# Expert weights in loads of 4 MB: slots side by side in one tensor, gate and up rows 4p + r

## The chip, the cores and the metric

One Trainium2 chip, one NeuronCore of it. Everything is fp32. The metric is the device time of one launch in microseconds, median of several runs; below, 1176.56 us for the kernel before.

## What is computed

One layer of a decoder for 256 tokens of width 1024: a combined input projection, sparse attention and a convolution branch, their mix, a layer norm, then a mixture of 32 experts of which each token takes 4, and a last gated embedding with a layer norm. The change touches the experts:

```python
def moe_ffn(h, w_router, b_router, w_gate_up, b_gate_up, w_down, b_down):
    ...
    top_vals, top_idx = lax.top_k(logits, TOP_K_EXPERTS)          # 4 of 32
    for e in range(N_EXPERTS):
        gu = t @ w_gate_up[e] + b_gate_up[e]                       # (1024, 2048)
        g, u = gu[:, :D_EXPERT], gu[:, D_EXPERT:]
        ...
        act = (u + 1) * (g * jax.nn.sigmoid(SWIGLU_ALPHA * g))
        y = act @ w_down[e] + b_down[e]                            # (1024, 1024)
        out = out + combine[:, e:e + 1].astype(t.dtype) * y
```

An expert's weights are 8 MiB of gate and up and 4 MiB of down, 384 MiB for all of them, each read once.

## The kernel before

**Stages.** The front (projection, attention, convolution, mix, router) reads its own weights through a ring of 12 chunks of 1 MiB (`ring`, `FRONT`, `w_view`, lines 287 to 313). Then the experts run one after the other, and last the gated embedding and the second layer norm.

**Slots.** An expert's weights come as six pairs of chunks (`CPE = 6`) of 2 MiB: c = 0 to 3 are 256 rows each of gate and up, c = 4 and 5 are 512 rows each of down. There are `ES = 11` slots of 2 MiB. Slots 0 to 5 are two chunks of `ring` each, slots 6 to 10 lie in `arena` (`extra`, at `EX + PAIR * (0, 1, 2, 4, 3)`), where the front's tensors lie before. The list in lines 323 to 332 hands slots out in a fixed turn, so load n takes the slot of load n - 11 (`last_in`); load `PP` has no bytes, and a slot is kept for a result there.

**Rows.** In `pair_source` (line 344) partition p gets rows 2p and 2p + 1 of a pair's 256 rows of gate and up, 16 KB that lie together, and rows 4p to 4p + 3 of 512 of down, also 16 KB.

**The gather.** Tokens of an expert are picked by a product with a one-hot matrix. The weights of these matmuls are columns of `x1`, in the order in which the rows of the expert's weights lie on the partitions: `x1_rows` (line 381) takes `x1` as 4 blocks of 128 x 2, so each weight load reads every second column. `gather` (line 399) does it for two experts at once, 16 matmuls, which are 32 records in the trace, after every odd expert; `first_gather` (line 408) for the first two experts, in pieces spread over the end of the router's work and expert 0; line 1170 for an expert with more than 64 tokens (two rounds).

**Who issues the loads.** SP's queue, in program order. While the front runs, `early` and `into_ring` (lines 563 to 597) fill the eleven slots as the front's tensors and chunks come free: load 9 ahead of chunk 25, then 0, 6, 1, half of 10, 2, 7, 3, 8, 4, 5 and the other half of 10. From line 604 on load n waits until TensorE has read load n - 11 (`pair_read`) and is issued; the loads in `PIECES` come in 2 or 4 parts as parts of the slot come free. `LAST` and the very last down pair are split too (lines 349 to 361). Each slot has a semaphore (`e_in`), and `filled[n]` is the count at which load n is there; TensorE waits for it in `pair` (line 949).

**TensorE in an expert** (`one_round`, line 1118): 64 records of gate and up (16 a pair), turning the sums, adding the last expert's rows to the total (`combine`, line 441), turning the gates or, after an odd expert, the next gather, and 32 records of down. `product` (line 423) issues both kinds. In experts 28 and 30 two embeddings (`embed`) lie between.

## Time and profile before

| | |
|---|---|
| three runs | 1176.01, 1176.56, 1176.84 us, median 1176.56 |
| the profiled execution | 1175.06 us |
| its span, first to last instruction | 1173.2 us |
| granted TensorE clock | 0.998 of full |
| TensorE matmul / weight load busy | 98% / 50% of the span |
| VectorE, ScalarE, GpSimd busy | 25%, 15%, 1% |
| DMA, packets of SP's queue | 90.8% of 16 engines' span |
| bytes | 448.16 MB, mean 382 GB/s |

A busy share is an average over stages with different limits, and matmuls are pipelined, with modelled ends: TensorE at 98% may still be waiting for short times between matmuls. Load and store shares say how full the 16 DMA engines were. What bounds a stage is read from that stage.

### The profile page before, as it was taken

How to read it: one execution, taken by the hardware profiler on the slowest of the kernel's cores; microseconds unless marked ns; L12 is line 12 of the kernel's file. 1: busy time of each engine (PE TensorE's matmuls, PEld its weight loads, DVE VectorE, ACT ScalarE, POOL GpSimd, SP SyncE). 2: the span in 40 equal slices, each digit the busy share in tenths (PEclk: the TensorE clock that was granted, in tenths of full speed). 3: DMA queues.
4: the chain of work that ended last, by engine and by line, in shares of the span. 5: the costliest groups of instructions: out<-in, count | busy, mean ns of one | idle time of the engine just before them, and what ended most of it. 6: DMA issues, size and time to landing. Idle time of an engine off the chain costs nothing.

```text
span 1173.2 us, 13754 instructions
## 1 busy us (share of the span) xinstructions
PE 1144.1 (98%) x5620; PEld 584.7 (50%) x5620; DVE 298.3 (25%) x775; ACT 173.7 (15%) x336; POOL 11.4 (1%) x26
## 2 busy tenths in 40 slices
PE   9999999999999999999999999999999898999997
PEld 8888888734344443434343344443434343434346
DVE  0639843521113111111111113111111111111125
ACT  1213230211111111101011011111101010111112
POOL 0110000000000000000000000000000000000000
PEclk9999999999999999999999999999999999999999
DMA  9996367699999999999999999999999999999970
GB/s 318 354 327 231 107 265 310 220 400 427 429 428 427 427 427 428 427 427 428 428 424 426 428 427 428 427 427 427 427 427 428 428 427 428 426 427 428 423 323 37
DMA packets 66808, 448.16 MB, mean 382 GB/s; under 512 B 7376, under 2 KB 36336, under 8 KB 41264
## 3 DMA queue, kind: packets, MB, share of 16 engines
q1 hardware_dynamic: 59184, 439.80, 90.8%
q10 hardware_dynamic: 7552, 7.38, 1.9%
q8 instruction: 49, 0.80, 0.3%
q14 instruction: 23, 0.19, 0.0%
HBM read 444.53 MB, written 2.62 MB: 381 GB/s over the span
## 4 chain that ended last, share of the span: by engine, by line
PE 80%; DMA 16%; DVE 2%; ACT 1%; issue 1%; SPq 0%; ACTq 0%; DVEq 0%
PE bank L426 47%; PE bank L696 10%; DMA ring<-in_w_gu 7%; DMA arena<-in_w_gu 7%; PE bank L446 5%; PE bank L403 4%; PE bank L843 2%; PE bank L856 2%; PE bank L1237 2%; PE bank L433 2%; ACT arena L1418 1%; PE bank L769 1%; PE bank L420 1%; DMA ring<-in_w_in 1%; PE bank L1110 1%
## 5 line engine op out<-in xcount | busy, mean ns | idle before, releaser
L426 PE MATMUL bank<-ring,arena 128*64 128x512 f32 x1712 | 377.6, 594 | 5.2 <-DMA ring<-in_w_gu 3.9
L426 PE MATMUL bank<-arena 128*64 128x512 f32 x1456 | 321.4, 594 | 8.7 <-DMA arena<-in_w_gu 7.8
L426 PEld LDWEIGHTS bank<-ring,arena 128*64 128x64 f32 x1712 | 123.8, 137 | 233.9 <-issue 219.4
L426 PEld LDWEIGHTS bank<-arena 128*64 128x64 f32 x1456 | 106.6, 137 | 207.3 <-issue 186.9
L466 DVE TENSOR_TENSOR arena<-bank,arena 128x512 f32<-128x512 f32 x33 | 22.8, 692 | 685.5 <-PE bank L433 685.5
L696 PE MATMUL bank<-arena,ring 128*128 128x256 f32 (+1 forms) x544 | 117.8, 377 | 0.2 <-DMA ring<-in_w_in 0.2
L696 PEld LDWEIGHTS bank<-arena,ring 128*128 128x128 f32 x544 | 102.0, 190 | 14.6 <-issue 1.0
L1418 ACT ACTIVATE arena<-bank 128x512 f32<-128x512 f32 x62 | 37.0, 597 | 397.7 <-PE bank L426 397.7
L446 PE MATMUL bank<-arena 64*128 64x512 f32 x272 | 67.8, 616 | 0.7 <-ACT arena L1421 0.7
L403 PEld LDWEIGHTS bank<-sel,arena 128*128 128x128 f32 x480 | 57.7, 196 | 11.4 <-issue 11.4
L403 PE MATMUL bank<-sel,arena 128*128 128x128 f32 x480 | 60.5, 285 | 0.0
L433 PEld LDWEIGHTS bank<-arena 128*128 128x128 f32 x264 | 36.8, 209 | 35.9 <-issue 24.3
L433 PE MATMUL bank<-arena 128*128 128x128 f32 x264 | 49.4, 310 | 2.3
L1421 ACT ACTIVATE arena<-bank 128x512 f32<-128x512 f32 x32 | 19.1, 597 | 210.3 <-PE bank L426 210.3
L1619 DVE SCALAR_TENSOR_TENSOR arena<-arena 128x256 f32<-128x256 f32 x120 | 48.5, 480 | 0.5 <-DVE arena L1619 0.2
L446 PEld LDWEIGHTS bank<-arena 64*128 64x128 f32 x272 | 23.4, 186 | 22.6 <-issue 17.1
L1306 ACT ACTIVATE arena<-bank,arena 128x256 f32<-128x256 f32 (+1 forms) x36 | 16.5, 466 | 95.6 <-PE bank L696 95.6
L486 DVE SCALAR_TENSOR_TENSOR arena<-arena 128x256 f32<-128x256 f32 x66 | 28.1, 425 | 4.0
L490 DVE TENSOR_TENSOR arena<-arena 128x256 f32<-128x256 f32 x66 | 28.1, 425 | 4.0
L856 PE MATMUL bank<-ring,arena 128*128 128x256 f32 x128 | 28.5, 380 | 0.0
L843 PE MATMUL bank<-arena,ring 128*128 128x256 f32 x128 | 27.9, 380 | 0.0
L472 DVE TENSOR_TENSOR arena<-bank,arena 128x256 f32<-128x256 f32 x66 | 27.6, 418 | 1.2 <-PE bank L433 1.2
(215 smaller groups left out, 527.4 us busy)
## 6 DMA issues: line engine op xcount, KB each, us to landing
ring<-in_w_gu SPq DMA_DIRECT2D x66, 2048.0 KB, 34.3
arena<-in_w_gu SPq DMA_DIRECT2D x58, 2048.0 KB, 35.3
ring<-in_w_dn SPq DMA_DIRECT2D x32, 2048.0 KB, 35.2
arena<-in_w_dn SPq DMA_DIRECT2D x27, 2048.0 KB, 34.0
ring<-in_w_in SPq DMA_DIRECT2D x19, 1024.0 KB, 12.7
ring<-in_w_gu SPq DMA_DIRECT2D x7, 1024.0 KB, 7.9
ring<-in_w_out SPq DMA_DIRECT2D x4, 1024.0 KB, 5.4
arena<-in_w_dn SPq DMA_DIRECT2D x4, 1024.0 KB, 23.8
```

What stands on the lines that cost most here:

```text
L403: mm = pe.matmul(bank[b + k // 4][:, (k % 4) * P:(k % 4 + 1) * P], x1_rows[:, t, k // 2, k % 2, :], sel[:, t, :, :], start=(t == 0), stop= ...
L426: mm = pe.matmul(to[half * CAP:(half + 1) * CAP, :], rows, w[:, half * 512:(half + 1) * 512], start=first, stop=last)
L433: mm = pe.transpose(to[:, j * P:(j + 1) * P], blocks[:, j, :], ident)
L446: mm = pe.matmul(total[t][n][:, :], G2[a:a + CAP, q, t * P:(t + 1) * P], rows[a:a + CAP, :], start=first, stop=last)
L472: i = nc.vector.tensor_tensor(by_bias(up[:, at], 4), by_bias(of_up[:, at], 4), bias_of(e, 1, 4 * j, 4), ALU.add)
L486: nc.vector.scalar_tensor_tensor(up[:, at], up[:, at], 1.0, gt[:, at], ALU.add, ALU.mult).then_inc(sw_step, 1 + 6 * skip * j)
L490: nc.vector.tensor_tensor(to[:, at], up[:, at], sg[:, at], ALU.mult).then_inc(act_ready, 1 + 2 * skip * j)
L696: mm = pe.matmul(bank[n % 4][:, lo:S], w[:, k, j * P:(j + 1) * P], xT_sb[:, k, lo:S], start=(k == 0), stop=(k == KD - 1))
L843: mm = pe.matmul(bank[n % 4][:, 0:S], w_view(i)[:, k, (c % 4) * P:(c % 4 + 1) * P], rhs[:, k, :], start=(k == 0), stop=(k == 3))
L856: mm = pe.matmul(mix_bank(t, j), merged[:, k, t * P:(t + 1) * P], w_view(25 + j)[:, k, :], start=(k == 0), stop=(k == KD - 1))
L1418: a.activation(rows, of[:, :], ACT.Identity).then_inc(h_out, 2 + 2 * j)
L1619: nc.vector.scalar_tensor_tensor(cy[:, a, :], u_sb[:, a, bass.ds(j, S)], dw[:, a, bass.ds(j, 1)], cy[:, a, :], ALU.mult, ALU.add).then_inc ...
```

## The change

It makes `ring` a part of `arena`: slots lie in one tensor in the order in which they are taken, so that slot i + 1 lies behind slot i everywhere but from slot 7 to slot 8. Gate and up rows are dealt out as those of down are: partition p has rows 4p to 4p + 3 of 512, 32 KB that lie together; pair c has the first or the second half of that, at 32 KB from partition to partition. The pairs c = 0 and 1, and c = 2 and 3, of experts 3 to 27 are loaded by one DMA of 4 MB where their slots are neighbours (`JOINED`): 45 such loads. A joined load waits until both slots are read, and both its pairs count as arrived when all of it is there. The gather takes `x1` as 2 blocks of 128 x 4. The first eleven slots are filled in another order: 7, 0, 1, half of 6, 3, 2, 4, 8, 5, 9, 10 and the other half of 6.

```diff
-        ring = sb("ring", [P, NS, SLOT])
-        arena = sb("arena", [P, 31575])
+        arena = sb("arena", [P, 31575 + NS * SLOT])
...
-        EX = 8192
-        extra = [view(EX + PAIR * j, PAIR) for j in (0, 1, 2, 4, 3)]
+        RING = 8192
+        ring = view(RING, NS * SLOT).rearrange("p (n s) -> p n s", n=NS)
+        EX = RING + NS * SLOT
...
-        PIECES = {5: 2, 10: 2, ES: 4, ES + 1: 2, ES + 2: 2, ES + 4: 2, ES + 5: 2}
-        slots, turn_of, slot_no, last_in, filled = list(range(ES)), [0] * ES, [], [], []
+        PIECES = {6: 2, 10: 2, ES: 4, ES + 1: 2, ES + 2: 2, ES + 4: 2, ES + 5: 2}
+        JOINED = [e * CPE + c for e in range(3, PP_E) for c in (0, 2) if (e * CPE + c) % ES != ES - 4]
+        slots, counts, slot_no, last_in, arrival = list(range(ES)), [0] * ES, [], [], []
         for n in range(NMP + CPE):
             i = slots.pop(0)
             last_in.append(max([m for m in range(n) if slot_no[m] == i], default=-1))
-            turn_of[i] += n != PP
             slot_no.append(i)
-            filled.append(16 * (turn_of[i] + sum(PIECES[m] - 1 for m in PIECES if m <= n and slot_no[m] == i)))
+            if n - 1 in JOINED:
+                arrival.append(arrival[n - 1])
+            else:
+                counts[i] += 16 * PIECES.get(n, 1)
+                arrival.append((i, counts[i]))
...
-        def slot_of(n):
-            i = slot_no[n]
-            if i >= NS // 2:
-                return extra[i - NS // 2]
-            i = 2 * (((NF - NS + 1) // 2 + i) % (NS // 2))
-            return ring[:, i:i + 2, :].rearrange("p a d -> p (a d)")
+        def slot_of(n, size=PAIR):
+
+            return view(RING + PAIR * (((NF - NS + 1) // 2 % (NS // 2) + slot_no[n]) % ES), size)
...
+        def rows_of_two(e, c):
+            return w_gu[bass.ds(e, 1), c // 2 * 512:(c // 2 + 1) * 512, :].rearrange("e (p r) d -> p (e r d)", r=4)
+
         def pair_source(e, c):
             if c < 4:
-                return w_gu[bass.ds(e, 1), c * 256:(c + 1) * 256, :].rearrange("e (p r) d -> p (e r d)", r=2)
+                return rows_of_two(e, c)[:, c % 2 * PAIR:(c % 2 + 1) * PAIR]
...
+            if n in JOINED:
+                sp.dma_start(slot_of(n, 2 * PAIR), rows_of_two(e, c)).then_inc(e_in[slot_no[n]], 16)
+                return
...
-        x1_rows = x1.rearrange("p t (c m r) -> p t c r m", c=4, r=2)
+        x1_rows = x1.rearrange("p t (c m r) -> p t c r m", c=2, r=4)
...
-                    mm = pe.matmul(bank[b + k // 4][:, (k % 4) * P:(k % 4 + 1) * P], x1_rows[:, t, k // 2, k % 2, :],
+                    mm = pe.matmul(bank[b + k // 4][:, (k % 4) * P:(k % 4 + 1) * P], x1_rows[:, t, k // 4, k % 4, :],
...
-                into_ring(0)
+                into_ring(0, 17)
                 sp.dma_start(wpp, w_pp.rearrange("(k p) d -> p k d", p=P)).then_inc(ple_in, 16)
+                into_ring(1, 19)
+                early(6, 1)
                 sp.wait_ge(pv_done, 8)
-                early(6)
-                into_ring(1)
-                early(10, 1)
-                into_ring(2)
+                early(3)
+                into_ring(2, 21)
                 sp.wait_ge(y_out, 8)
-                early(7)
-                into_ring(3)
+                early(4)
+                into_ring(8, 23)
                 sp.wait_ge(merged_ready, 8)
-                early(8)
-                into_ring(4)
-                into_ring(5, 0)
-                into_ring(5, 1)
-                early(10, 0)
+                early(5)
+                into_ring(9, 25)
+                into_ring(10, 27, 0)
+                into_ring(10, 27, 1)
+                early(6, 0)
...
-                    if n == PP:
+                    if n == PP or n - 1 in JOINED:
                         continue
                     sp.wait_ge(*pair_read(last_in[n]))
+                    if n in JOINED:
+                        sp.wait_ge(*pair_read(last_in[n + 1]))
                     load_pair(sp, n, *divmod(n - (1 if n > PP else 0), CPE))
...
                 def pair(n):
-                    pe.wait_ge(e_in[slot_no[n]], filled[n])
+                    i, count = arrival[n]
+                    pe.wait_ge(e_in[i], count)
                     return slot_of(n)
```

## Rows read from the trace of the kernel before

**Rows 1.** The page, the 40 slices of the span: DMA share and rate.
```profile
DMA  9996367699999999999999999999999999999970
GB/s 318 354 327 231 107 265 310 220 400 427 429 428 427 427 427 428 427 427 428 428 424 426 428 427 428 427 427 427 427 427 428 428 427 428 426 427 428 423 323 37
```
**Rows 2.** Stretches: length, then PE, PEld, DVE, ACT, POOL busy, PEclk, DMA share, GB/s.
```profile
324.00:378.00 54.00, 53.85 (x266) 22.62 (x266) 10.07 (x28) 6.69 (x12) 0.00 (x0) 1.00 1.01 428
...
537.00:591.00 54.00, 52.88 (x259) 21.36 (x259) 9.01 (x26) 6.70 (x12) 0.00 (x0) 1.00 1.01 427
...
930.00:977.00 47.00, 42.64 (x210) 17.06 (x206) 4.72 (x11) 5.08 (x9) 0.00 (x0) 1.00 1.01 428
977.00:1036.00 59.00, 54.43 (x264) 21.37 (x264) 9.55 (x27) 6.69 (x12) 0.00 (x0) 1.00 1.01 427
1036.00:1095.00 59.00, 57.17 (x270) 22.61 (x270) 9.64 (x27) 7.89 (x14) 0.00 (x0) 1.00 1.01 428
```
**Rows 3.** Timeline of PE: start us, us, line, operation, count [idle before <- releaser].
```profile
324.33 1.99 PE L446 MATMUL bank<-arena 64*128 64x512 f32 x8
...
377.54 1.99 PE L446 MATMUL bank<-arena 64*128 64x512 f32 x8
...
1030.71 3.65 PE L426 MATMUL bank<-arena 128*64 128x512 f32 x16 [0.48 <-DMA arena<-in_w_gu]
...
1089.46 3.65 PE L426 MATMUL bank<-arena 128*64 128x512 f32 x16 [0.49 <-DMA arena<-in_w_gu]
```
**Rows 4.** The view of the DMA queues, at 42 to 80 us and at 300 to 600 us.
```profile
DMA packets 13215, 13.22 MB, mean 348 GB/s; under 512 B 209, under 2 KB 13211, under 8 KB 13211
...
DMA packets 8806, 128.25 MB, mean 427 GB/s; under 512 B 976, under 2 KB 976, under 8 KB 976
```
**Rows 5.** SP's loads 14, 16 (second half), 19, 21, 10 (half), 27: issue, then landing.
```profile
L367 SPq DMA_DIRECT2D ring<-in_w_gu x1: 327/327/327, 245.2 to 245.2; - x1
DMA to landing us min/median/max: 10.4/10.4/10.4
...
L365 SPq DMA_DIRECT2D ring<-in_w_dn x1: 328/328/328, 256.0 to 256.0; - x1
DMA to landing us min/median/max: 9.5/9.5/9.5
...
L367 SPq DMA_DIRECT2D arena<-in_w_gu x1: 328/328/328, 266.3 to 266.3; - x1
DMA to landing us min/median/max: 14.9/14.9/14.9
...
L367 SPq DMA_DIRECT2D arena<-in_w_gu x1: 328/328/328, 280.7 to 280.7; - x1
DMA to landing us min/median/max: 10.3/10.3/10.3
...
L365 SPq DMA_DIRECT2D ring<-in_w_dn x1: 327/327/327, 221.5 to 221.5; - x1
DMA to landing us min/median/max: 4.9/4.9/4.9
...
L367 SPq DMA_DIRECT2D ring<-in_w_gu x1: 328/328/328, 305.8 to 305.8; - x1
DMA to landing us min/median/max: 14.5/14.5/14.5
```
**Rows 6.** Timeline of PE: the matmuls of contiguous, step 2 and step 4 weights.
```profile
214.36 1.87 PE L874 MATMUL bank<-wr_sb,arena 128*128 128x32 f32 x16
...
225.11 0.41 PE L911 MATMUL bank<-arena 128*128 128x32 f32 x2
...
226.34 1.21 PE L413 MATMUL bank<-sel,arena 128*128 128x128 f32 x8
...
326.25 4.04 PE L403 MATMUL bank<-sel,arena 128*128 128x128 f32 x32
...
1135.41 2.53 PE L1227 MATMUL bank<-arena 128*128 128x128 f32 x16
```

More of the change, by code:

```diff
@@ L202, in program @@
         stats4 = view(o + 1895, 48).rearrange("p (t a b) -> p t a b", t=NT, a=4)
-        assert o + 1943 + 512 <= 31575
+        assert o + 1943 + 512 <= 31575 + NS * SLOT
         relb_sb = sb("relb_sb", [NB, H])
@@ L351, in load_pair @@
                 to = slot_of(n).rearrange("p (r d) -> p r d", r=2)
-                of = w_gu[bass.ds(e, 1), c * 256:(c + 1) * 256, :].rearrange("e (p r) d -> p (e r) d", r=2)
+                of = pair_source(e, c).rearrange("p (r d) -> p r d", r=2)
                 sp.dma_start(to[:, :, 0:1024], of[:, :, 0:1024]).then_inc(e_in[slot_no[n]], 16)
@@ L412, in first_gather @@
                     pe.wait_ge(x1_ready, 3 + k // 4)
-                mm = pe.matmul(bank[2 - 2 * t + k // 4][:, (k % 4) * P:(k % 4 + 1) * P], x1_rows[:, t, k // 2, k % 2, :],
+                mm = pe.matmul(bank[2 - 2 * t + k // 4][:, (k % 4) * P:(k % 4 + 1) * P], x1_rows[:, t, k // 4, k % 4, :],
                                sel[:, t, :, :], start=True, stop=True)
@@ L564, in early, with into_ring @@
                     load_pair(sp, n, n // CPE, n % CPE, piece)
-                def into_ring(n, piece=None):
-                    i = NF - NS + 2 * n
+                def into_ring(n, i, piece=None):
                     sp.wait_ge(*front_used(i + (0 if piece == 0 else 1)))
@@ L575, in _ @@
                         sp.wait_ge(lg_out, 8)
-                        early(9)
+                        early(7)
                     if i >= NS:
@@ L1169, in two_rounds @@
                         for t in range(NT):
-                            mm = pe.matmul(gate_turned[:, k * CAP:(k + 1) * CAP], x1_rows[:, t, k // 2, k % 2, :],
+                            mm = pe.matmul(gate_turned[:, k * CAP:(k + 1) * CAP], x1_rows[:, t, k // 4, k % 4, :],
                                            sel_b[:, t, :], start=(t == 0), stop=(t == NT - 1))
@@ L1254, in weights @@
                         n = NMP + c
-                        pe.wait_ge(e_in[slot_no[n]], r * 16 + filled[n])
+                        i, count = arrival[n]
+                        pe.wait_ge(e_in[i], r * 16 + count)
                         return slot_of(n)
```

## The prediction

> **What bounds the kernel now.** I read the 40 slices of the page first. From the tenth slice (about 264 us) to slice 38 the DMA row stands at 9 and the GB/s row at 423 to 429: the 32 experts' weights arrive in one unbroken stream [rows 1]. The PE row shows 9 there too, so the stretches decide which of the two is the limit. At 324 to 378 us TensorE works 53.85 of 54 us; at 930 to 1095 it stands still for 4.4, 4.6 and 1.8 us, and before that for 1.1 us at 537 to 591, while the DMA share never leaves 1.01 [rows 2]. The timeline says why: two experts cost TensorE 53.2 us when their weights are there (L446 at 324.33 and again at 377.54), but two experts' weights, 24 MiB, take 58.75 us to arrive (the waits for the last gate-up pair end at 1030.71 and 1089.46), or 4.896 us per 2 MiB load [rows 3]. TensorE starts the experts with eleven full slots and eats that lead until the first wait, in the stretch that ends at 591 us, regains some in the one expert with two rounds, and waits again from the stretch at 930 us on [rows 2]. So the end is set by: when the stream starts, its holes and its rate, with a tail behind it. TensorE has about 12 us of slack (1.1 + 4.4 + 4.6 + 1.8) and is the second limit, close behind.
>
> **The change part by part.** The tensor that holds the slots and the order in which the first eleven are filled move no bytes and free no slot sooner; all eleven are still there when the first expert starts, so both cost nothing (cover: the DMA's idle time before that; without it, a late first pair would cost up to its 4.9 us). Semaphores: the second pair of a joined load waits again for a count already reached, in a sequencer that is not the limit. Four things are left.
>
> *1. Fewer, longer rows.* 45 loads of 4 MiB (gate-up pairs of experts 3 to 27, without the five that begin at slot 7) take the place of 90 of 2 MiB: 188.7 MB, 90 x 4.896 = 441 us of the stream. A partition's piece of a load becomes one 32 KB row instead of two of 16 KB. What a row costs beside its bytes: at 42 to 80 us 13,006 rows of about 1 KB take 38 x 16 / 13,006 = 46.7 ns each of one DMA engine; at 300 to 600 us 7,830 rows of 16 KB take 300 x 16 / 7,830 = 613 ns [rows 4]. A straight line through both gives 37.75 ns per KB and 9 ns per row. The nearest rows are the two loads that came in 8 KB rows: they landed at 265.5, 9.9 us behind the 255.6 of the load before, where two loads in 16 KB rows take 9.8 [rows 5]; 0.1 over 16 more rows per engine is 2 to 14 ns with the rounding. A joined load saves 8 rows per engine. Bounds: 0 (a 32 KB row may be cut in two) and 9 x 8 x 45 = 3.3 us. I take 7 ns, near the upper end, because rows of 8 KB, the nearest in length, still seem to pay about 8: **-2.5 us**.
>
> The rows show what a row costs, not why. The Trainium skill (DMA: Bandwidth & Descriptors, "Why small descriptors are slow") puts it at a fixed overhead of about 3 cycles per packet, one cycle carrying 32 B; by that 16 KB is 512 + 3 cycles, halving it saves 0.29% of 441 us, an estimate of 1.3 us, and my sum would end 1.2 us later. The trace doesn't agree at 1 KB, where the line through rows 4 has 9 ns beside 38 and that rule would have 9%.
>
> *2. A hole in the stream.* A joined load needs two neighbouring slots free. The first (loads 20 and 21, expert 3, c = 2 and 3) meets a short queue. Now load 20 is issued when expert 1's last gate-up pair is read, and load 21 at 280.7, after turning, combining, gathering and the first down pair. Load 19, issued at 266.3, lands at 281.2, load 21 at 291.0 [rows 5]. Changed, nothing is issued between 19 and 280.7, so the DMA engines run dry. On an idle queue 1 MB landed after 4.9 us [rows 5], so about 2.5 us lie between issue and the flow of bytes: the pair lands at 280.7 + 2.5 + 9.8 = 293.0, 2.0 us late. Every later load is behind it: nothing gives this back. Later joined loads have the same gap of release, but TensorE gains 0.46 us on the stream with every load and the queue grows: 10.3 us from issue to landing at 280.7, 14.5 at 305.8 [rows 5]. I count one hole. Bounds 1.4 to 5 us (an overlap of issue and drain; a second hole).
>
> *3. The gather reads x1 at a step of 4 instead of 2.* Rows 4p + r make every weight load of a gather pick every fourth column. Back to back, a contiguous load costs 1.87 us / 16, at most 117 ns (L874); step 2, 4.04 / 32 = 126 (L403); step 4 in the transposes at L1227, 2.53 / 16 = 158, with short waits in it [rows 6]. With the pipeline's fill taken off the last is about 142 and the middle 124, so I take +18 ns per record, 0 to +35 as bounds. A gather has 32 records: +0.6 us, 15 times, 9 us on TensorE, inside its slack of 12. What isn't hidden: the first gathers. Twelve records end just ahead of the mask that L911 takes at 225.11; eight run on the path at 226.34 [rows 6], and eight more inside expert 0. All delay the first releases of slots: 8 x 18 + 8 x 18 ns + about 0.1 = 0.4 us. And expert 1's gather lies ahead of the release that the hole waits for: +0.6. The pair then lands at 293.0 + 0.4 + 0.6 = 294.0: points 2 and 3 together cost **+3.0 us** against 291.0.
>
> *4. TensorE behind the stream at the end.* With pairs arriving in twos it starts the first of two when the second is there, one pair (3.5 us) later. Joins stop at expert 27, and 4 experts x 29.4 us of stream less 4 x 26.6 of work less two embeddings of 3.4 and one slower gather leave 3.8 us to catch up. Nearly all is regained: **+0.2 us**, bounds 0 and 1.5.
>
> **Sum:** -2.5 + 3.0 + 0.2 = +0.7 us. The profiled execution took 1175.06 us (span 1173.2 and 1.9 around it), 1.5 under the median of the three runs, 1176.56; the prediction goes by the median: **1177.3 us**, no difference that a measurement can tell (0.2%, 2.35 us).
>
> **Rivals.**
> *A, the saving wins (0.27).* Longer rows save the full 9 ns and the end of each load (its 16 semaphore packets are halved too) some more, while step 4 costs the weight loads little (L1227 may be slow for its waits). Then -3.3 - 1 + 2.0 + 0.2 = -2 to -3: 1174. For it: the stream covers 441 us, so 1% more rate is already 4.4 us. Against: rows 4 leave no room for 1%.
>
> *B, the saving isn't there and the hole decides (0.18).* If a 32 KB row moves as two of 16 KB, the 3.2 us of points 2 to 4 stand alone: 1179.8, slower. The point from which it decides is a saving under (3.2 - 2.35) / 45 = 19 ns per joined load, where rows 4 promise up to 72. A second hole, at the load that is issued at 305.8 [rows 5], would add 1 to 3.
>
> *C, the reading pattern is slower (0.10).* Before, the 128 rows of a gate-up load start 16 KB apart; afterwards 32 KB, also in the loads that aren't joined. No row of this trace has that pitch; priced by the stream, 1% of all 128 gate-up loads (627 us) is 6 us: 1183. The Trainium skill (the same page, "Latency and other measured facts") has rates falling at row pitches of large powers of two, with a small loss at 512 KiB and more above; by it 32 KB should be free, and no run here shows it yet.
>
> *D, TensorE becomes the limit.* Past 0.8 us per gather (12 us over 15) the slack is gone; at 1.2 us each, 37 ns per record, the end moves 2 us more: 1179. It needs the worst end of point 3; I give it 0.05 and count it with slower.
>
> **Chances.** The forecast itself has 0.40. Of A's 0.27, 0.25 lie more than 0.2% below, the rest within; B, C and D are slower by more. So faster 0.25, within 0.2% 0.42, slower 0.33. The range reaches to A with a little over (1172.8) and through B towards C (1182.0).
>
> **What would show it.** In the stretches the stream's rate between 300 and 900 us: 428 to 430 GB/s says point 1 is right, 427 says B, under 425 C. In DMA packets, 128 per joined load rather than 256. In the issue view, a 4 MB load about 281.7 landing about 294, and a dip in GB/s at 281 to 284. L403's 32 records in 4.5 us instead of 4.0. Waits of TensorE for DMA shrink from 12 to about 3 us plus what the joins add. The prediction is wrong if holes appear at later joined loads, or if TensorE never waits at 1000 to 1095.

## The result, and the profile after

The changed kernel takes 1225.33 us (median of 4 runs, 1224.51 to 1226.62), the kernel before 1176.28 beside it (1175.01 to 1176.84): ratio 1.042, 95% interval 1.0401 to 1.0438, so 49 us slower. The forecast was 1177.3 us with a range up to 1182.0. The span of the profiled execution is 1224.9 us, where it was 1173.2.

The page of the changed kernel: span, busy times, slices, packets, the chain, the gather's two groups, the new loads.

```profile
span 1224.9 us, 13754 instructions
...
PE 1207.0 (99%) x5620; PEld 650.6 (53%) x5620; DVE 298.3 (24%) x775; ACT 173.8 (14%) x336; POOL 11.4 (1%) x26
...
PEclk9999999999999999999998999999999999999999
DMA  9996475797999999999997679999999999999920
GB/s 321 351 300 221 157 294 211 285 406 318 429 432 431 431 428 429 429 430 430 427 430 320 280 320 428 425 429 429 429 429 430 429 431 428 427 427 429 424 96 35
DMA packets 60328, 448.16 MB, mean 366 GB/s; under 512 B 6656, under 2 KB 35616, under 8 KB 40544
...
PE 96%; ACT 2%; DVE 1%; DMA 1%; issue 1%; SPq 0%; ACTq 0%; DVEq 0%
...
L411 PEld LDWEIGHTS bank<-sel,arena 128*128 128x128 f32 x480 | 113.1, 329 | 11.4 <-issue 11.4
...
L411 PE MATMUL bank<-sel,arena 128*128 128x128 f32 x480 | 116.0, 400 | 0.0
...
arena<-in_w_gu SPq DMA_DIRECT2D x45, 4096.0 KB, 22.2
```

Three things stand out against before. The number of instructions is the same to the last one, 13,754, and TensorE's matmuls are busy for 1207.0 us instead of 1144.1, 62.9 more: the same work takes longer. The stream now has weak slices from the tenth on (318, then 320, 280, 320), where [rows 1] had 423 to 429 up to the 38th. They aren't due to the joined loads: the kernel before with nothing changed but the gather's step, below, joins none and has 385, then 338, 246, 357 in the same slices. The likely reason is that a TensorE that is behind frees slots later, and the loads wait for them. And the chain that ends last is 96% TensorE and 1% DMA; before it was 80% and 16%. L411 is the gather's line (L403 before), where the kernel before had 60.5 us in the same 480 records, 285 ns each.

The stretches of the changed kernel (columns as in [rows 2]), the first three and the last two at the same times as there.

```profile
324.00:378.00 54.00, 53.85 (x248) 24.87 (x246) 9.39 (x25) 6.70 (x12) 0.00 (x0) 1.00 1.00 427
537.00:591.00 54.00, 53.85 (x248) 24.48 (x245) 6.80 (x19) 5.93 (x11) 0.00 (x0) 1.00 1.01 432
...
930.00:977.00 47.00, 46.85 (x218) 22.09 (x216) 9.21 (x25) 6.10 (x11) 0.00 (x0) 1.00 1.00 426
977.00:1036.00 59.00, 58.85 (x272) 26.56 (x270) 9.56 (x26) 6.70 (x12) 0.00 (x0) 1.00 1.01 430
1036.00:1095.00 59.00, 58.85 (x264) 26.61 (x262) 9.39 (x25) 7.89 (x14) 0.00 (x0) 1.00 1.00 426
...
280.00:290.00 10.00, 10.00 (x46) 6.03 (x47) 0.00 (x0) 1.20 (x2) 0.00 (x0) 1.00 0.31 108
```

TensorE no longer waits in any of them: 0.15 us a stretch are left, where it stood still for 4.4, 4.6 and 1.8 us at 930 to 1095. The last line is the hole ahead of the first joined load, deeper than forecast: the slow gathers move its issue from the forecast 281.7 to 287.84, and in the run of step 4 without joined loads this stretch has 306 GB/s.

The weight loads are the place. First the gather's line in the changed kernel, then in the kernel before (min/median/max of one, in ns).

```profile
L411 PEld LDWEIGHTS bank<-sel,arena x480: 307/329/330, 276.4 to 1123.0; 128*128 128x128 f32 x160
L411 PE MATMUL bank<-sel,arena x480: 397/397/499, 276.4 to 1123.1; 128*128 128x128 f32 x160
```

```profile
L403 PEld LDWEIGHTS bank<-sel,arena x480: 193/196/198, 273.0 to 1070.7; 128*128 128x128 f32 x160
L403 PE MATMUL bank<-sel,arena x480: 280/282/387, 273.0 to 1070.9; 128*128 128x128 f32 x160
```

A load of 128 x 128 weights takes 329 ns at a step of 4 columns and 196 at a step of 2: 133 ns more, of which a record of the gather, one behind the other, takes 115. The timeline of TensorE shows it, at the first gathers, the first expert and the last gather.

```profile
222.66 1.18 PE L421 MATMUL bank<-sel,arena 128*128 128x128 f32 x4
...
224.03 3.04 PE L421 MATMUL bank<-sel,arena 128*128 128x128 f32 x12
...
228.02 1.94 PE L421 MATMUL bank<-sel,arena 128*128 128x128 f32 x8
...
230.91 1.51 PE L434 MATMUL bank<-arena 128*64 128x512 f32 x6 [0.51 <-DVE arena L1798]
...
1115.76 7.73 PE L411 MATMUL bank<-sel,arena 128*128 128x128 f32 x32
```

Thirty-two records take 7.73 us where [rows 6] had 4.04, and the eight ahead of the first expert 1.94 instead of 1.21; the first expert starts at 230.91 instead of 228.49. **The account:** 15 gathers at +3.7 us are 55.4; the gather of the expert with two rounds and the 32 records of the first gathers add 3.7 each (115 ns per record). That makes 62.8 us of added work. TensorE's idle time falls from 29.1 us (1173.2 - 1144.1) to 17.9, so 11.2 are swallowed, and the growth of its busy time less that, 62.9 - 11.2 = 51.7, is the growth of the span.

That 62.8 and 62.9 are so close is chance, because two more terms lie in the same sum. One adds. From 635 to 655 us the granted clock is 0.74 of full on the mean, and at its lower level, 0.50 or 1.2 GHz, from 646 to 652:

```profile
646.00:652.00 6.00, 6.00 (x18) 2.83 (x19) 0.00 (x0) 0.60 (x1) 0.00 (x0) 0.50 0.99 426
```

It is the one expert with two rounds: 16 records that begin at 634.77 take 5.35 us instead of 3.65, and the 112 from 647.71 take 26.74 instead of 24.25, some 4 us in all. What lets it fall is open. TensorE stands still for 1.82 us ahead of these records, but in the kernel before it stands still for 2.06 at the same place, and the clock stays at 1.00; step 4 in the kernel before has the same 0.74.

The other takes away. A wait for DMA costs TensorE more than the idle time that the profile shows, because it breaks a run of matmuls: in the kernel before, 16 records behind a wait are busy for 3.65 us, while two unbroken runs say that 16 more add only (13.95 - 7.09) / 2 = 3.43.

```profile
661.26 13.95 PE L426 MATMUL bank<-ring,arena 128*64 128x512 f32 x64
...
682.53 7.09 PE L426 MATMUL bank<-arena 128*64 128x512 f32 x32
```

The 13 such waits of the kernel before stand for 11.7 us idle, and by this estimate for 2.9 more that are counted as busy. The changed kernel has none of them. So the estimate is 62.8 + 4.2 - 2.9 = 64.1 for the 62.9 measured, and the slack is 14.6 us, not 12; the experiments below measure 13 to 14.

### The profile page after: what moved, and what is told of

It is laid out like the page before. It is cut to its first block, busy times and chain, and to the rows that moved or that the text cites. A ratio compares the mean times of both kernels' runs of the same rounds, so it can differ in the third digit from the quotient of the medians.

```text
span 1224.9 us, 13754 instructions
## 1 busy us (share of the span) xinstructions
PE 1207.0 (99%) x5620; PEld 650.6 (53%) x5620; DVE 298.3 (24%) x775; ACT 173.8 (14%) x336; POOL 11.4 (1%) x26
## 4 chain that ended last, share of the span: by engine, by line
PE 96%; ACT 2%; DVE 1%; DMA 1%; issue 1%; SPq 0%; ACTq 0%; DVEq 0%
PE bank L434 56%; PE bank L705 10%; PE bank L411 9%; PE bank L454 5%; PE bank L852 2%; PE bank L865 2%; PE bank L1247 2%; PE bank L441 2%; ACT arena L1429 1%; PE bank L778 1%; PE bank L428 1%; DMA arena<-in_w_in 1%; PE bank L421 1%; PE bank L1180 1%; PE bank L1120 1%
## 5 line engine op out<-in xcount | busy, mean ns | idle before, releaser
L434 PE MATMUL bank<-arena 128*64 128x512 f32 x3168 | 696.1, 597 | 2.3 <-DVE arena L498 1.7
L434 PEld LDWEIGHTS bank<-arena 128*64 128x64 f32 x3168 | 235.5, 137 | 425.8 <-issue 415.7
L411 PEld LDWEIGHTS bank<-sel,arena 128*128 128x128 f32 x480 | 113.1, 329 | 11.4 <-issue 11.4
L705 PE MATMUL bank<-arena 128*128 128x256 f32 (+1 forms) x544 | 117.8, 377 | 0.8 <-DMA arena<-in_w_in 0.8
L411 PE MATMUL bank<-sel,arena 128*128 128x128 f32 x480 | 116.0, 400 | 0.0
L705 PEld LDWEIGHTS bank<-arena 128*128 128x128 f32 x544 | 101.9, 190 | 15.3 <-DMA arena<-in_w_in 1.4
L1429 ACT ACTIVATE arena<-bank 128x512 f32<-128x512 f32 x62 | 37.0, 597 | 383.2 <-PE bank L434 383.2
L441 PEld LDWEIGHTS bank<-arena 128*128 128x128 f32 x264 | 36.8, 208 | 35.9 <-issue 24.3
L1432 ACT ACTIVATE arena<-bank 128x512 f32<-128x512 f32 x32 | 19.1, 597 | 210.4 <-PE bank L434 210.4
L550 ACT ACTIVATE arena<-bank 128x512 f32<-128x512 f32 x30 | 17.9, 597 | 117.1 <-PE bank L411 117.1
L865 PE MATMUL bank<-arena 128*128 128x256 f32 x128 | 28.5, 380 | 0.0
L852 PE MATMUL bank<-arena 128*128 128x256 f32 x128 | 27.9, 380 | 0.0
L480 DVE TENSOR_TENSOR arena<-bank,arena 128x256 f32<-128x256 f32 x66 | 27.6, 417 | 1.2 <-PE bank L441 1.2
L1247 PE MATMUL bank<-arena 128*128 128x256 f32 x128 | 27.8, 379 | 0.0
```

Source lines behind the costliest of these rows:

```text
L411: mm = pe.matmul(bank[b + k // 4][:, (k % 4) * P:(k % 4 + 1) * P], x1_rows[:, t, k // 4, k % 4, :], sel[:, t, :, :], start=(t == 0), stop= ...
L434: mm = pe.matmul(to[half * CAP:(half + 1) * CAP, :], rows, w[:, half * 512:(half + 1) * 512], start=first, stop=last)
L441: mm = pe.transpose(to[:, j * P:(j + 1) * P], blocks[:, j, :], ident)
L705: mm = pe.matmul(bank[n % 4][:, lo:S], w[:, k, j * P:(j + 1) * P], xT_sb[:, k, lo:S], start=(k == 0), stop=(k == KD - 1))
L852: mm = pe.matmul(bank[n % 4][:, 0:S], w_view(i)[:, k, (c % 4) * P:(c % 4 + 1) * P], rhs[:, k, :], start=(k == 0), stop=(k == 3))
L865: mm = pe.matmul(mix_bank(t, j), merged[:, k, t * P:(t + 1) * P], w_view(25 + j)[:, k, :], start=(k == 0), stop=(k == KD - 1))
```

## The experiments

**Back to step 2, all else as changed.** The gather reads wrong columns for these rows of weights, so the experts' products are those of other pairs; the work is the same.

```diff
-        x1_rows = x1.rearrange("p t (c m r) -> p t c r m", c=2, r=4)
+        x1_rows = x1.rearrange("p t (c m r) -> p t c r m", c=4, r=2)
```

(and `k // 2, k % 2` as indices in the three gathers)

> The changed kernel in all but one thing: the gather's weights are read at a step of 2 columns of x1, as before the change, so the experts get columns of x1 that don't belong to their rows (that part of the computation is changed). Theory S (the step is the whole loss): a gather falls from 7.7 us back to 4.0, its weight loads from 329 ns to 196, TensorE waits for DMA again, and the time is that of the kernel before give or take what my points 1 and 2 make of it, -3.3 us for 45 loads of longer rows and +2.0 for one hole: about 1175, 1171 to 1180. Rival D (loads of 4 MB, holes or the pitch of 32 KB carry a good part of the 49 us): the time stays well above 1185, with the DMA rate below 425 GB/s or several holes.

1176.5 us, 11 runs, ratio to the kernel before 1.0006 (0.9997 to 1.0016), span 1174.7. The 49 us are gone, and the gather's weight loads are at 196 ns. What is left is the change without step 4, and it is the case that my sum of points 1, 2 and 4 was about. The stretches around the first joined load:

```profile
270.00:280.00 10.00, 9.93 (x62) 6.57 (x62) 4.07 (x10) 2.42 (x4) 0.00 (x0) 1.00 0.82 348
280.00:290.00 10.00, 10.00 (x50) 3.29 (x48) 0.00 (x0) 0.87 (x2) 0.00 (x0) 1.00 0.79 316
290.00:300.00 10.00, 9.92 (x50) 3.76 (x46) 0.56 (x1) 1.19 (x2) 0.00 (x0) 1.00 1.02 434
```

and the load itself:

```profile
L373 SPq DMA_DIRECT2D arena<-in_w_gu x1: 327/327/327, 281.1 to 281.1; - x1
...
DMA to landing us min/median/max: 13.3/13.3/13.3
```

It lands at 294.4, 3.4 us behind the 291.0 of [rows 5] (0.4 of it because the experts start 0.4 later in this trace, at 228.85), and from 300 to 600 us the stream runs at 429 GB/s with 6111 packets, where [rows 4] had 427 and 8806.

**Step 4 alone, in the kernel before.** The mirror image: the kernel before with `c=2, r=4` in `x1_rows` and nothing else (so again columns that don't belong to the rows).

> The kernel before with one thing changed: the gather's weights are read at a step of 4 (columns of x1 that don't belong to the rows, so that part of the computation is changed). Theory S: weight loads of the gather take 329 ns, 15 gathers cost 3.7 us more each (55 us), the two-round one 3.7 and the first pieces about 2.4 on the front; 12 us of waiting for DMA are swallowed: 1176.3 + 55 + 3.7 + 2.4 - 12 = 1225, 1220 to 1230. Rival D: it stays within some 10 us of the kernel before. Rival T (the slots in one tensor, with other addresses, make the loads slow): 1176, since the tensors are those of before.

1225.58 us, 4 runs, ratio 1.0418 (1.0402 to 1.0433), weight loads at 329 ns, TensorE busy 1207.5 us, span 1224.9. So the gather's step is the whole of the loss: it is enough by itself, and without it nothing is lost. What the 32 KB rows could bring is not seen here either, since TensorE sets the end.

**No joined load, step 2.**

```diff
-        JOINED = [e * CPE + c for e in range(3, PP_E) for c in (0, 2) if (e * CPE + c) % ES != ES - 4]
+        JOINED = []
```

> As e1, and no load is joined: all loads are 2 MB, gate and up rows of 16 KB at a pitch of 32 KB. It prices the pitch, the one tensor and the order of filling together. If these are free, 1176.3 within 1 us and 427 GB/s at 300 to 600 us. If the pitch costs (my rival C), 1% of the gate-up stream is 6 us: 1182.

1175.56 us, 11 runs, ratio 0.9999 (0.999 to 1.0008), 427 GB/s. One tensor for the slots, the other order of filling and the 32 KB from partition to partition cost nothing that a measurement can tell. Rival C falls. The Trainium skill (DMA: Bandwidth & Descriptors, "Latency and other measured facts") gives rates for row pitches from 512 KiB up, with a small loss at 512 KiB. This run agrees as far as it goes: at 32 KB there is none.

**Joined from expert 5 on, step 2.** `range(5, PP_E)` instead of `range(3, PP_E)`: the loads of experts 3 and 4, issued while the queue is short, stay single.

> As e1, with the joined loads from expert 5 on instead of 3. If my point 2 is right (one hole, at the first joined load, because the queue is short then), the dip in the DMA rate at 281 to 290 us is gone and the time is 2 to 3 us under e1: the saving of 42 joined loads at 72 ns, 3.0 us, is left alone, so 1173.3. If longer rows save nothing, it equals e3. If joined loads open other holes, it stays at e1.

1174.15 us, 11 runs, ratio 0.9985 (0.9976 to 0.9994), span 1172.4. There is no hole (1.00 of DMA share and 424 GB/s at 280 to 290), and the run is the first below the kernel before. But the last gate and up pair lands 3.2 us earlier than before, while TensorE begins to turn the last expert's sums only 0.8 us earlier (1119.33 instead of 1120.16): from 1036 to 1095 it works 58.75 of 59 us.

**What a step costs.** In the kernel before, the eight sets of columns of each gather are read at steps of 1 to 8 from the start of `x1` (so the gathered tokens are not the reference's), each on a line of its own.

```diff
-                    mm = pe.matmul(bank[b + k // 4][:, (k % 4) * P:(k % 4 + 1) * P], x1_rows[:, t, k // 2, k % 2, :],
-                                   sel[:, t, :, :], start=(t == 0), stop=(t == NT - 1))
+                    to, one = bank[b + k // 4][:, (k % 4) * P:(k % 4 + 1) * P], dict(start=(t == 0), stop=(t == NT - 1))
+                    by = lambda step, first=0: x1[:, t, 0:128 * step].rearrange("p (m r) -> p r m", r=step)[:, first, :]
+                    if k == 0:
+                        mm = pe.matmul(to, by(1), sel[:, t, :, :], **one)
...
+                    if k == 7:
+                        mm = pe.matmul(to, by(8), sel[:, t, :, :], **one)
```

> The kernel before, in which the eight column sets of every gather (not the first ones) are read at steps 1, 2, 2 (from an odd column), 3, 4, 4 (from column 2), 5 and 8, a source line each (other columns than the rows need, so that part of the computation is changed). Theory L (a weight load pays by 16-byte pieces of a row, four fp32 to a piece, and hides the cost as long as two elements come from one): steps 1 and 2 about 190 and 196 ns, step 3 between 196 and 329 (1.33 elements per piece), steps 4, 5 and 8 all 329, the same from an odd column. Rival P (the cost grows with the step, by the bytes passed over): 5 and 8 clearly above 4. Rival E (only powers of two from 4 on, by banks): 3 and 5 stay near 196.

The weight loads by line: step 1, step 2, step 2 from the second column, step 3, step 4, step 4 from the third column, step 5, step 8.

```profile
L406 PEld LDWEIGHTS bank<-sel,arena x60: 186/190/192, 273.2 to 1082.1; 128*128 128x128 f32 x60
L408 PEld LDWEIGHTS bank<-sel,arena x60: 196/196/198, 273.6 to 1082.5; 128*128 128x128 f32 x60
L410 PEld LDWEIGHTS bank<-sel,arena x60: 196/196/197, 274.1 to 1083.0; 128*128 128x128 f32 x60
L412 PEld LDWEIGHTS bank<-sel,arena x60: 252/261/263, 274.6 to 1083.6; 128*128 128x128 f32 x60
L414 PEld LDWEIGHTS bank<-sel,arena x60: 317/330/330, 275.3 to 1084.5; 128*128 128x128 f32 x60
L416 PEld LDWEIGHTS bank<-sel,arena x60: 330/330/330, 276.2 to 1085.4; 128*128 128x128 f32 x60
L418 PEld LDWEIGHTS bank<-sel,arena x60: 317/318/321, 277.1 to 1086.3; 128*128 128x128 f32 x60
L420 PEld LDWEIGHTS bank<-sel,arena x60: 332/336/336, 278.0 to 1087.3; 128*128 128x128 f32 x60
```

No slope with the step, but a knee: 1 and 2 are alike (190, 196), 3 lies between (261), from 4 on all are alike (318 to 336). This fits a price that is paid per 16 bytes of a partition that are touched, though only fp32 was run: at steps 1 and 2 each such piece gives four or two fp32 values, at step 4 and more only one, at step 3 one or two. A price per byte of distance, or one for powers of two, doesn't fit 318 at step 5. The Trainium skill (Advanced Engine Details and Errata, "SBUF Cachelines") has this rule: lines of 16 bytes, and at least two hits on each are needed for full speed. The rows agree. The Trainium skill (SBUF — State Buffer, "Door 1: The DMA port swizzle") also has a sentence by which fp32 can be read at a step of 4 for free. The measurement decides, and it says no: 330 ns against 190. The one run took 1190.94 us.

**A quarter and a half of the gather at step 4.** Two, then four of the eight sets of columns, in the kernel before.

```diff
+                    rows = x1.rearrange("p t (c m r) -> p t c r m", c=2, r=4)[:, t, k // 4, k % 4, :] if k < 2 else x1_rows[:, t, k // 2, k % 2, :]
```

(`k < 4` for the half; the sets at step 4 are other columns than the weights' rows)

> The kernel before with step 4 in two of the eight column sets of a gather (columns that don't belong to the rows, so that part is changed). It tests the slack of 12 us: each gather costs 0.93 us more, 13.9 us over 15. If TensorE's waits for DMA swallow 12 of them, the time is 2 us up, 1178, 1176 to 1180. If TensorE had been the limit all along (its busy share of 98%), all 14 us show: 1190.

> As e6, with four of the eight column sets: 1.85 us more per gather, 27.8 us. With a slack of 12 us: 1176 + 16 = 1192, 1189 to 1195. Without slack 1204.

The quarter took 1175.66 us (10 runs, ratio 1.0003, 0.9994 to 1.0012), though its gathers cost TensorE 74.4 us instead of 60.5. The half took 1189.39 (4 runs, ratio 1.0121, 1.0106 to 1.0136), 14.0 above the 1175.38 of the kernel before beside it. Its gathers add 15 x 16 x 115 ns = 27.6 us, so about 13.6 are swallowed; the quarter's 13.9 vanish within 0.3. The slack is 13 to 14 us, near the 14.6 estimated above, and TensorE's time beyond it goes to the end one for one (13.8 us of gathers more in the half than in the quarter, 13.7 us later). Three stretches of the quarter show it just used up, with one wait of 0.98 us left; its gathers cost 13.9 us more, its busy time grew by 10.9, which is the same 3 us of waits that were counted as busy:

```profile
930.00:977.00 47.00, 46.93 (x230) 20.16 (x230) 6.74 (x19) 4.87 (x9) 0.00 (x0) 1.00 1.01 428
977.00:1036.00 59.00, 58.61 (x284) 24.52 (x281) 9.68 (x26) 7.89 (x14) 0.00 (x0) 1.00 1.01 427
1036.00:1095.00 59.00, 57.86 (x272) 23.83 (x271) 9.63 (x26) 7.89 (x14) 0.00 (x0) 1.00 1.01 427
```

**x1 stored as it is read.** VectorE writes `x1` in the order r, m within each 512, so the gathers read it contiguously; rows of weights, slots and joins (from expert 5 on) as changed. It computes the whole of the reference, as the next one does.

```diff
-        x1_rows = x1.rearrange("p t (c m r) -> p t c r m", c=2, r=4)
+        scaled = view(o + 1204, 512)
+        x1_rows = x1.rearrange("p t (c r m) -> p t c r m", c=2, r=4)
...
-                    nc.vector.scalar_tensor_tensor(x1[:, t, at], x1[:, t, at], rstd[:, t:t + 1], lnb1[:, at],
+                    nc.vector.scalar_tensor_tensor(x1_rows[:, t, j].rearrange("p r m -> p m r"),
+                                                   scaled.rearrange("p (m r) -> p m r", r=4), rstd[:, t:t + 1],
```

> The changed kernel, complete: the last step of the layer norm writes x1 with its columns in the order (block, r, m), so that the gather of columns 4m + r reads 128 neighbouring columns, and the residual reads them back in that order; joined loads from expert 5 on. Theory S and L: weight loads of the gather near 190 ns, gathers of 3.5 us, the DMA stream is the limit again, with the saving of e4: 1174, and 0.3 less for shorter first gathers, if VectorE's four scattered writes and four scattered reads of 512 columns cost no more than now (745 and 682 ns). If VectorE pays for the scatter as TensorE does, each costs some 0.5 us more on the path and it ends at 1176 to 1178.

1176.3 us, 11 runs, ratio 1.0006 (0.9997 to 1.0015). The gather is fast again, and VectorE pays: its shifts, which now write each value 128 columns from the last, take 1.11 us instead of 0.75, the tail's four products 3.95 instead of 2.48. The first expert's matmul begins at 229.72, 1.2 us late, which moves everything behind it; that and the tail take what the joined loads bring.

**The same, with VectorE reading at step 4 and writing contiguously**, and two residual operations moved ahead.

> The turned x1 again (gather's weights contiguous, 4 MB loads from expert 5), with VectorE reading at a step of 4 and writing contiguously where it wrote scattered before, the last product of the layer norm reading x1 contiguously as it lies, and two residual operations moved ahead of the first scale and shift. In the run before, the shifts took 1.10 to 1.12 us instead of 0.75, the four operations of the tail 3.95 instead of 2.48 us, and the first expert's matmul began at 229.72 instead of 228.49. Theory S (a scattered write is what costs VectorE): the shifts are back at 0.75 to 0.85, the tail at about 2.5, the first expert begins by 228.8; the end is 1.3 + 0.9 us sooner than 1176.3: about 1174.1. Theory R (a strided access costs on either side alike): shifts 1.1, tail 3.9, and the time stays at 1176. Gathers' weight loads at step 1 cost TensorE under 200 ns per record in both.

1175.85 us, 11 runs, ratio 1.0 (0.9991 to 1.0009). A miss for theory S, a hit for R. The shift in the two runs and in the kernel before:

```profile
L1730 DVE SCALAR_TENSOR_TENSOR arena<-arena x4: 1105/1113/1124, 208.2 to 229.5; 128x512 f32<-128x512 f32 x4
```

```profile
L1730 DVE SCALAR_TENSOR_TENSOR arena<-arena x4: 1146/1148/1152, 212.8 to 228.8; 128x512 f32<-128x512 f32 x4
```

```profile
L1717 DVE SCALAR_TENSOR_TENSOR arena<-arena x4: 741/749/752, 208.0 to 228.3; 128x512 f32<-128x512 f32 x4
```

A strided read costs VectorE as much as a scattered write; the first expert began at 229.02.

**Joins end at expert 23, step 2** (columns again not the rows'). `range(5, 24)` instead of `range(5, PP_E)`.

> Step 2, joined loads of experts 5 to 23 instead of 5 to 27 (about 8 joins fewer). Theory T (TensorE's lag behind a stream of pairs in twos eats the gain at the end: the last loads landed 3.2 us earlier with joins to expert 27, the end came only 0.8 to 2 us earlier): the stream gives up 8 x 0.07 = 0.6 us, TensorE has four experts more to catch up, and the end comes at 1173.3 to 1174.0, not later than the 1174.15 with joins to 27. TensorE waits for DMA again after 1060 us. Rival V (TensorE's whole work since the first wait, not the lag, is what binds: a total of work that no order shortens): the end stays within 0.3 us of 1174.15 while the last loads land 0.6 us later, and TensorE has no wait longer than 0.3 us from 1036 to 1095. Rival W (the stream alone sets the end): 0.6 us later, 1174.8.

1173.31 us, 11 runs, ratio 0.9981 (0.9972 to 0.999): the fastest of all, with 35 joined loads instead of 42. Theory T holds, V and W fall. TensorE waits for a pair again at the end:

```profile
1086.94 3.65 PE L434 MATMUL bank<-arena 128*64 128x512 f32 x16 [0.49 <-DMA arena<-in_w_gu]
...
1120.45 0.74 PE L441 MATMUL bank<-arena 128*128 128x128 f32 x4
```

where [rows 3] had 1089.46, and in the kernel before the last turning of the sums began at 1122.91: 2.5 us earlier in this trace. The gain over the run with joins to expert 27 is 0.8 us in the medians, within the spread of either, so its size is rough; the waits are what tells the theories apart.

**x1 in pairs.** If TensorE needs two values of each 16 bytes, a step of 2 is enough, and VectorE may ask for no more: `x1` is stored with rows 0 and 1 of all partitions two by two, then rows 2 and 3. A second temporary lies on the input of the last embedding, so part of that embedding is computed from other values.

```diff
+        x1_rows = x1.rearrange("p t (c h m l) -> p t c h m l", c=2, h=2, l=2)
...
+                    for h in range(2):
+                        nc.vector.scalar_tensor_tensor(x1_rows[:, t, j, h],
+                                                       scaled[j].rearrange("p (m h l) -> p h m l", h=2, l=2)[:, h],
```

> x1 is stored in blocks of pairs: of the four rows of a partition, rows 0 and 1 of all partitions lie next to each other two by two, then rows 2 and 3, so the gather's weight loads read at step 2 (two values of every four), where step 4 cost 329 ns and step 2 costs 196 to 197. VectorE reads and writes in runs of two values, in two operations of 256 columns instead of one of 512, with two temporaries instead of one. Joined loads of experts 5 to 23. Theory Q (what costs VectorE is the same as what costs TensorE's weight load: fewer than two values used of four that lie together): a shift's two halves take 0.42 to 0.45 us each, about 0.8 together, the tail's four products 2.7 to 3.0 us instead of 3.9, the first expert's matmul begins by 228.8, and the end comes 1.0 us sooner at the front and 1.2 at the tail than with the single strided accesses, and as in the run with joins to expert 23: 1173.3 to 1174.3. Theory Z (VectorE pays for every row that isn't contiguous): halves of 0.55 to 0.6 us each, tail 3.9 or more, 1175.5 to 1176.5. Gathers' weight loads at 196 ns in both.

1174.84 us, 11 runs, ratio 0.9991 (0.9982 to 1.0).

```profile
L1732 DVE SCALAR_TENSOR_TENSOR arena<-arena x8: 474/480/490, 208.5 to 229.5; 128x256 f32<-128x256 f32 x8
```

Half a shift takes 0.48 us, the two together 0.87 back to back, the tail's eight products 2.74. The kernel before has contiguous operations of the same form and size, 256 columns and a factor per partition:

```profile
L1619 DVE SCALAR_TENSOR_TENSOR arena<-arena 128x256 f32<-128x256 f32 x120 | 48.5, 480 | 0.5 <-DVE arena L1619 0.2
```

They take the same 0.48. So theory Q holds for VectorE's price, if not for the end that it named: runs of two at a distance of four cost nothing, and the 0.12 us more than the 0.75 of a whole shift go with the second instruction. The forecast 0.42 to 0.45 fits operations of 425 ns (L486 of the kernel before) that have a constant in place of the factor. The shifts of the first half of the tokens lay ahead of the residuals that TensorE waits for: its first expert began at 229.33.

**Pairs, complete.** One temporary, residuals ahead; the whole of the reference.

> The kernel with pairs, which computes the whole of the reference: one temporary instead of two, and the two residual operations of the second half of the tokens moved ahead of the first scale and shift, so that the longer shifts of the first half (0.87 us instead of 0.75) no longer lie ahead of them. Joined loads of experts 5 to 23. Sum against the run with joins to 23 and step 2 as it was: the shift of the second half of the tokens on the path +0.15, the tail's products 2.74 instead of 2.48: +0.25. So 1173.3 + 0.4 = 1173.7 if the sum holds, at most 1174.2: 0.15 to 0.2% under the kernel before. Rival: what the run with two temporaries gave, 1174.84, came from a stream that started 0.8 us later for another reason than the shifts; then this one stays at 1174.8.

1175.72 us, 11 runs, ratio 0.9991 (0.9982 to 1.0) to 1176.41 beside it. A miss: 0.7 us below the kernel before, not 2.7. The sum's own terms came nearly as written (+0.24 at the front for +0.15, 2.74 in the tail), and the end did not follow:

```profile
228.81 3.65 PE L435 MATMUL bank<-arena 128*64 128x512 f32 x16 [0.51 <-DVE arena L1804]
...
1087.96 3.65 PE L435 MATMUL bank<-arena 128*64 128x512 f32 x16 [0.53 <-DMA arena<-in_w_gu]
...
1113.47 6.23 PE L435 MATMUL bank<-arena 128*64 128x512 f32 x28 [0.75 <-DMA arena<-in_w_gu]
...
1137.51 27.79 PE L1248 MATMUL bank<-arena 128*128 128x256 f32 x128
```

The first expert began at 228.81, 0.24 us behind the 228.57 of the run with joins to 23 and step 2, but the stream was 1.0 us behind at 1087.96. The difference arises between 230 and 240 us (127 to 346 GB/s in its three stretches, 184 to 379 in that run). Why is open: the loads there are issued 0.24 us later, no more, no run varied them, and single executions of the kernel before differ by 2.5 us beside this run (1175.17 to 1177.69), so chance isn't ruled out. It is the rival that I had written down, and still no version that computes the reference beats the kernel before by more than the measurement can tell.

## Why the prediction was wrong

**Point 3, the step that failed.** I put +18 ns on a record, 0 to +35 as bounds; it was +133 ns on a weight load and +115 on a record. The order of thought was right (weights at a wider step, 15 gathers on TensorE, slack behind them, a delay ahead of the first expert), only the price was off by a factor of six, beyond its bound by three. Two choices did that.

I took transposes for the nearest rows of step 4. They are another operation, and pay less. But even they, read rightly, would have warned me: I divided 2.53 us of matmul time by 16 and called the rest waits, where the weight loads have rows of their own. In the kernel before:

```profile
L1227 PEld LDWEIGHTS bank<-arena x16: 195/210/221, 1135.4 to 1137.5; 128*128 128x128 f32 x16
```

```profile
L866 PEld LDWEIGHTS bank<-arena x16: 138/141/223, 206.1 to 222.0; 128*128 128x128 f32 x16
```

L1227 reads at a step of 4, L866 contiguously: +69 ns. With that as a bound, a gather is 32 x 69 = 2.2 us longer, 15 of them 33 us, far past the slack of 12, and rival D would have had to be the top of the range: 1176.6 + 33 - 12 = some 1198. Even my own bound of +35 ns breaks the slack, 35 x 32 x 15 = 16.8 us, yet point 3 calls it inside on the strength of the middle value. The other choice was a straight line through contiguous, step 2 and step 4. Between 1 and 2 hardly anything happens (190 and 196 ns), then a knee. The Trainium skill states it (Advanced Engine Details and Errata, "SBUF Cachelines", above); the prediction draws on what the skill has on DMA alone, though the part of the change that is read by an engine is the gather.

**Rival D, 0.05,** was the mechanism. Its condition, more than 0.8 us per gather, and its working hold: 15 x 3.7 = 55.4 less 12, and 2.4 at the front and 3.7 for the two rounds, is 49.5. Measured were 49 in the medians and 51.7 between the two profiled executions, with a slack of 13 to 14 rather than 12 and 4 us of lower clock in the same sum. I had bounded it by point 3's own upper end, so its chance fell with that price. Its price was a slip besides: at 1.2 us per gather, 15 x 1.2 - 12 is 6 us and not 2, so even by the prediction's own terms D stood at some 1182 to 1183, not 1179.

**Point 1 holds.** 429 GB/s and 6107 packets from 300 to 600 us, one packet per row of 32 KB. The run with joins from expert 5 to 27 lands the last gate and up pair 3.2 us earlier than the kernel before, with 42 joined loads: 3.2 / 42 / 8 = 9.5 ns per row, the straight line's 9 rather than the 7 that I took. The size is rough: the run with joins to 23 lands it 2.4 us earlier with 35, and the run with no joined load 1.4 us later, so beside that one the 42 spare 4.6. Nor do the runs tell a row's price from what a whole load less spares; the packets fall by 144 per joined load, 128 rows and 16 others. By the Trainium skill's 3 cycles per packet (DMA: Bandwidth & Descriptors, "Why small descriptors are slow"), an estimate of 1.3 us for 45 loads, it would be 1.2 us for these 42. The traces have more.

**Point 2 holds in its place, not in its size.** The first joined load met an empty queue. A 4 MB load takes 13.3 us there (13.2 in the changed kernel), 3.5 beyond the 9.8 of its bytes, where I took 2.5 from a 1 MB load; so 3.4 us late instead of 2.0, 0.4 of it from the later start. With point 1 that leaves the change without step 4 where it is measured, 1176.5 with 1175.56 for no joins.

**Point 4 was too small.** I let TensorE catch up in four experts. The run with joins to expert 27 has it busy to 58.75 of 59 us at the end; joins to 23 gave waits again and 0.8 us. Not all of the 3.2 us that the stream gained reached the end: 1.7 in the medians (1174.15 and 1175.81 beside it), 0.8 in the two traces.

**What should have shown it right or wrong:** the forecast was wrong if TensorE never waits from 1000 to 1095 us, and it never does. The other sign, holes at later joined loads, would have misled: the weak slices of the changed kernel stand in the run of step 4 without joined loads too. Points 1, 2 and 4, corrected to -3.2 to -3.6, +3.4 and about +1, come to about +1; the change without step 4 measured +0.7 (1176.5 and 1175.81 beside it), no difference that a measurement can tell. Point 3 makes the 49 us.

## What to carry over

When an access pattern of an engine changes, read the duration of the instruction that makes the access (here the weight loads, not the matmuls) in contiguous and strided rows of the same trace, and expect a knee, not a slope: fp32 weights at a step of up to 2 are free, from 4 on they cost 1.7 times as much. Compare the worst price with the slack of the engine behind the stream before giving it a low chance: a stage with 12 us of slack over 15 repetitions can bear 0.8 us each. Idle time behind waits is a lower bound of that slack: here it was 12, and 13 to 14 were swallowed. And a layout that suits DMA must be paid by someone who reads it: turning it in the producer cost as much here as the longer rows brought, and grouping by two values instead of four lowered that price to that of a second instruction.

## What the runs showed of the hardware

- Weight loads of 128 x 128 fp32 in a matmul: 190 ns at step 1, 196 at 2, 261 at 3, 330 at 4, 318 at 5, 336 at 8. In a transpose 141 at step 1 and 210 at 4.
- VectorE over 512 fp32 columns: 0.75 us contiguous, 1.11 when it writes at a step of 128, 1.15 when it reads at a step of 4; 256 columns 0.48, contiguous or read in runs of two at a distance of four.
- A 4 MB load on an idle queue takes 13.2 to 13.3 us, 3.5 more than its share of the full stream.
- The granted clock was 0.74 on the mean from 635 to 655 us in the changed kernel, 0.50 (1.2 GHz) from 646 to 652, and cost 4 us; TensorE had stood still for 1.8 us. The kernel before kept 1.00 at the same expert behind 2.1 us.
- A wait for DMA costs TensorE some 0.2 us beyond the idle time shown (estimate from 3.65 us for 16 records behind a wait, 3.43 for 16 more in an unbroken run).
